# Where the split weights of paired pieces lie in their ring: 64 bytes below the plain ones, or 64 bytes above

## The reference

```
h = x @ w_up                                  # 2048 -> 2 * 5632
hc = conv_b + sum(conv_w[kk] * hp[:, kk:kk + S] for kk in range(3))
f = (silu(gate) * up) @ w_down                # 5632 -> 2048
x = layernorm(ALPHA * x + f)
```

## The kernel before

| operand | behind | at modulo 256 |
| --- | --- | --- |
| plain granules (`w_hi`, `w_lo`) | | 192 |
| `ffn_xT`, the moving operand of the feature stages | | 128 |
| `ffn_act`, `pairs_x`, `tokens_xT`, stationary in the token stages | a margin of 64 bytes | 192 |
| `next_held_w_hi/lo`, held granules | a margin of 64 bytes | 192 |
| `diff_split_...`, operands of the cross-attention in layer 1 | a margin of 64 bytes | 192 |
| `memory_memT` | margins of 64 and 192 bytes | 128 |
| `up_pair_w_hi/lo`, two granules kept apart | a margin of 64 and one of 32 bytes | 224 |

## Time and profile before

### The profile page before, as it was taken

How to read it: one execution, slowest core, us unless ns; L and a number is a source line. 1 busy time by engine, 2 the same in 40 slices (tenths; PEclk the granted TensorE clock), 3 DMA queues, 4 the chain that set the end, 5 groups by cost and what they waited for, 6 DMA issues and landing times.

```text
span 2082.7 us, 38940 instructions
## 1 busy us (share of the span) xinstructions
PE 2077.0 (100%) x14554; PEld 1916.0 (92%) x14554; DVE 1529.5 (73%) x2716; ACT 1215.3 (58%) x2222; POOL 2.7 (0%) x12
## 2 busy tenths in 40 slices
PE   9999999999999999999999999999999999999999
PEld 8999889999999998888888888899999999988887
DVE  6767777767766669888766558667766677688888
ACT  5645566556555555655656666566555565555654
POOL 0000000000000000000000000000000000000000
PEclk9999999999999999999999999999999999999999
DMA  9655666565655556556554454745655656565554
GB/s 348 235 176 167 210 219 213 188 201 181 201 190 192 196 176 212 183 201 223 192 168 165 167 177 167 256 153 193 201 192 191 198 185 198 169 218 181 204 202 162
DMA packets 201631, 408.97 MB, mean 196 GB/s; under 512 B 7616, under 2 KB 9152, under 8 KB 200768
## 3 DMA queue, kind: packets, MB, share of 16 engines
q1 hardware_dynamic: 201392, 407.45, 57.5%
q10 hardware_dynamic: 144, 0.26, 0.0%
HBM read 404.53 MB, written 3.15 MB: 196 GB/s over the span
## 4 chain that ended last, share of the span: by engine, by line
PE 98%; DVE 1%; DMA 0%; SPq 0%; ACT 0%; issue 0%
PE acc L1846 32%; PE acc L1848 32%; PE acc L1847 32%; PE acc L2177 0%; DMA head_first<-in_first 0%; PE acc L2151 0%; PE acc L1959 0%; PE acc L2201 0%; PE acc L1952 0%; PE acc L2209 0%; DVE x_tok L1817 0%; PE acc L2047 0%; SPq L563 0%; DVE x_tok L1822 0%; PE acc L2261 0%; PE acc L2282 0%
## 5 line engine op out<-in xcount | busy, mean ns | idle before, releaser
L1105 DVE TENSOR_TENSOR w_lo<-raw,w_hi 128x512 fp32r<-128x512 f32 x1330 | 878.5, 686 | 398.3 <-ACT w_hi L662 394.5
L662 ACT ACTIVATE w_hi<-raw 128x512 fp32r<-128x512 f32 x1330 | 804.6, 629 | 559.3 <-PE acc L1848 549.1
L1846 PE MATMUL acc<-ffn_xT,w_hi 128*128 128x256 f32 x2920 | 806.7, 276 | 0.0
L1847 PE MATMUL acc<-ffn_xT,w_hi 128*128 128x256 f32 x2920 | 806.2, 276 | 0.0
L1848 PE MATMUL acc<-ffn_xT,w_lo 128*128 128x256 f32 x2920 | 806.2, 276 | 0.0
L1847 PEld LDWEIGHTS acc<-ffn_xT,w_hi 128*128 128x128 f32 x2920 | 548.4, 188 | 0.1
L1846 PEld LDWEIGHTS acc<-ffn_xT,w_hi 128*128 128x128 f32 x2920 | 548.2, 188 | 0.1
L1848 PEld LDWEIGHTS acc<-ffn_xT,w_lo 128*128 128x128 f32 x2920 | 548.1, 188 | 0.0
L1846 PE MATMUL acc<-w_hi,ffn_act 128*128 128x512 f32 (+1 forms) x642 | 234.6, 365 | 0.0
L1847 PE MATMUL acc<-w_lo,ffn_act 128*128 128x512 f32 (+1 forms) x642 | 234.6, 365 | 0.0
L1848 PE MATMUL acc<-w_hi,ffn_act 128*128 128x512 f32 (+1 forms) x642 | 234.5, 365 | 0.0
(11 more groups left out here) (318 smaller groups left out, 1949.4 us busy)
## 6 DMA issues: line engine op xcount, KB each, us to landing
raw<-in_ffn_w_up SPq DMA_DIRECT2D x172, 1024.0 KB, 5.0
raw<-in_ffn_w_down SPq DMA_DIRECT2D x88, 1024.0 KB, 5.1
raw<-in_diff_w_in SPq DMA_DIRECT2D x38, 1024.0 KB, 5.4
raw<-in_w_out SPq DMA_DIRECT2D x32, 1024.0 KB, 5.1
raw<-in_pool_w_in SPq DMA_DIRECT2D x16, 1024.0 KB, 5.1
raw<-in_mem_w_kv SPq DMA_DIRECT2D x12, 1024.0 KB, 12.3
next_from_raw<-in_ffn_w_up SPq DMA_DIRECT2D x4, 1024.0 KB, 10.2
head_first<-in_first SPq DMA_DIRECT2D x5, 768.0 KB, 11.0
```

The costliest lines, as they stand in the source:

```text
L662: nc.scalar.activation(hi, raw_place(st, c, k, j), ACT.Copy).then_inc(hi_made, 1)
L1105: nc.vector.tensor_tensor(lo, raw_place(st, c, k, j), hi.bitcast(F32), ALU.subtract).then_inc(lo_made, 1)
L1846: pe.matmul(out, w[0], x[0], start=start, stop=False, skip_group_check=True)
L1847: pe.matmul(out, w[0], x[1], start=False, stop=False, skip_group_check=True)
```

## The change

Before, all units of a paired piece lie 64 bytes below the usual places, at 128 modulo 256, and so does the last plain granule in front of the piece, which would otherwise overlap the first unit. After, the first unit of a paired piece lies at the usual place (192), the six others 64 bytes above theirs (256, that is 0 modulo 256), and every plain granule at the usual place. The gap that stood ahead of the ring's first slot stands behind its last one. The size of the ring, the order of the instructions and their number on every engine stay the same; addresses and the counts in ACT's waits (`frees`) are what differs.

```
-SLOT_AT = [CHUNK * SLOT_ORDER.index(i) + 64 * sum(at in GAP_SLOTS for at in SLOT_ORDER[:SLOT_ORDER.index(i) + 1]) for i in range(HALVES * PIECE)]
+SLOT_AT = [CHUNK * SLOT_ORDER.index(i) + 64 * sum(at in GAP_SLOTS for at in SLOT_ORDER[1:SLOT_ORDER.index(i) + 1]) for i in range(HALVES * PIECE)]
...
-        self.places = [(SLOT_AT[(first + n + (skip if c > 0 else 0)) % len(SLOT_AT)] - (UNIT_SHIFT if self.lower(c, k, n - starts[c * pieces + k]) else 0))
+        self.places = [(SLOT_AT[(first + n + (skip if c > 0 else 0)) % len(SLOT_AT)] + (UNIT_SHIFT if self.higher(c, k, n - starts[c * pieces + k]) else 0))
...
-    def lower(self, c, k, j):
-
-        return self.paired(c, k) or (j == PIECE - 1 and k + 1 < self.pieces and self.paired(c, k + 1))
+    def higher(self, c, k, j):
+
+        return self.paired(c, k) and j > 0
```

## The result

| | before | after |
| --- | --- | --- |
| median of 20 runs, us | 2084.99 (2084.16 to 2086.72) | 2088.88 (2087.66 to 2089.98) |
| the profiled execution, its own time | 2084.49 | 2088.98 |
| its span | 2082.7 | 2087.2 |

The ratio is 1.0017, with a 95% interval of 1.0011 to 1.0024: 3.5 us slower (2.3 to 5.0); the medians in the table are 3.9 us apart. I had forecast 0.5 us faster. The time lies in the range of 8 in 10 that I gave but far outside the one around the forecast itself (2084.3 to 2086.1), and it is where the second rival put it (+3.2 us, 2088.8); the sign of the forecast was wrong.

What follows compares the result with a forecast made beforehand. PE was taken to bound the kernel, by matmul pace or a new wait. The terms -0.92 + 0.23 + 0.2 gave -0.5 us from 2085.57, so 2085.1 us (2084.3 to 2086.1); 8 in 10 range 2083.9 to 2091.1.

Steps and rivals of the forecast that it cites:

- the second rival: Paired pieces: units at 0 never fall into step behind a first unit at 120 ns; +3.2 us, 2088.8; chance 0.18.
- What bounds the kernel: Whole kernel: PE is busy throughout, so only the pace of matmuls or a new wait of PE can move the end.
- The last plain granule: Ahead of each pair, back from 128 to 192: 1.40 to 1.36 us, 23 times, 0.92 us less.
- The first unit: First six matmuls of each pair, from 128 to 192: 0.71 us against 0.70, 23 times, +0.23 us (0 to +0.5).
- The six other units: 828 matmuls in the pairs, from 128 to 0: pace taken as still 113.3 ns, 0 us; bounds -1.4 to +5.5.
- The seams: Switch from unit 0 to 1 and exit to a plain granule: 0.01 us per piece together, +0.2 us (-0.2 to +0.7).
- The waits of ACT: Some units in the ring written one use of PE later, others earlier; at the tightest place hidden by DVE's queue; 0 us.
- the first rival: Paired pieces: the units at 0 fall to 120 ns; +5.3 us, 2090.9; chance 0.20.
- The signs named in advance: Piece 0 of chunk 1: granule 1.36 us, first unit 0.71, 36 matmuls 4.08 and 276 ns in flight; longer means a rival.
- One sign against the mechanism: Stages outside the two `w_down` changing their pace would show the mechanism wrong, as would a plain granule keeping 1.40 at 192.

Runs made afterwards that it cites:

- the first experiment: Changed kernel with the six other units of each pair at 128 instead of 0, first units and waits as changed; median 2084.63 us, ratio 1.0001.
- second experiment: Changed kernel with the first unit of each pair at 0 as well, so all seven units at 0; 2088.84 us, ratio 1.0018.
- third experiment: Changed kernel with all seven units of a pair at 128 and every plain granule at 192; 2088.12 us, ratio 1.0015.
- kernel six: Changed kernel with unit places set by piece; in piece 3 the first unit at 192, the others at 96; one run, 2087.95 us.

## Why the prediction was wrong

**What bounds the kernel, and that only pace or a new wait can matter:** right. The loss is pace, 3.80 us of it inside the two `w_down`.

**The last plain granule, -0.92 us:** right, 1.40 to 1.36.

**The first unit, +0.23 us:** right in kind, 0.71 as the row of six matmuls at 192 in layer 1 had it, which is entered in the same way. The size was at the upper end of its bounds (0 to +0.5): the unit before takes 0.69 in most of the pieces, not the 0.70 of the piece that was shown, and the mean over the 23 goes from 0.692 to 0.713 us, 0.5 us in all.

**The six other units, 0 taken within -1.4 to +5.5:** this is the step that failed. I took 113.3 ns because 128 and 0 lie 64 bytes on either side of the stationary operand. That symmetry does not exist: at 0 the pace is 117.8, behind each of the four entries that were tried. 828 matmuls by 4.5 ns are 3.7 us, and the term had been put at nothing. The bounds held; the choice within them rested on no row.

**The seams, +0.2 us:** less than half of what was measured, and within its ends: by the means over the 23 pieces the exit goes from 1.375 to 1.393 us, 0.4 us in all, the granule behind it and the switch from the first unit to the second add 0.1 us or less each.

**The waits of ACT, 0:** right for PE, which had none in `w_down`; the first experiment kept all the counts and lost nothing. ACT's longest wait grew to 2.1 us, where I had named 1.0 us more at the tightest place.

**The second rival** had the pace (117.7, from the earlier trace rows) and nearly the sum, and the wrong reason; that its 2088.8 us and the measured 2088.88 agree is luck. Its +3.2 us, like the +5.3 of the first rival, leaves out the first unit's own +0.23. It said that the units at 0 stay out of step because of the 120 ns ahead of them. The same 120 ns ahead of units at 128 bring them *into* step, and units at 0 are at 117.8 with nothing of the kind ahead (second experiment). But what its row showed, two steady paces at one placement, is real, for 128: that row, and the 113.3 of the pairs, were the two.

**The kernel before owed its 113.3 to the granule that looked like a cost.** Its last plain granule at 128 takes 0.04 us more, and I counted its removal as the change's gain, which it is. But with the units at 128 it is also what sets their pace: without it they run at 117.7 (third experiment), 0.17 us per pair. A price and what it buys were read as if they were apart.

**The signs named in advance.** The plain granule at 1.36, the first unit at 0.71, 4.24 us for the 36 and 280 ns in flight are those of the second rival. One sign against the mechanism, a stage outside `w_down` that changes its pace, also came: the first stage did, but not by the change (last section).

By the rule of the Trainium skill ("TensorE: Matmul & The Clock Gate", Step-by-step) that the two operands have independent read ports, all eight kernels and both originals would have one time as far as PE goes; they span 2084.6 to 2090.7 us with the same number of instructions on every engine. What happens between the two operands inside the chip, the runs do not show.

**Open.** Whether the paces follow the distance between the two operands or the place of each: in the pairs the stationary one was at 192 throughout. The distance alone does not seem to fix them: stationary 224 with moving 128 runs at 120, stationary 192 with moving 96, the same 96 bytes apart, at 117.2 (kernel six); but they were entered differently, and 96 may have two paces as well. Nor does anything here show the addresses themselves: they come from the sizes in the source, and if the allocation began elsewhere, all places would move by the same amount. And what in the stream decides between 113.3 and 117.7; I have which entries lead where and no mechanism. Whether the accesses of ACT, DVE and the DMAs to the same memory have a part was not tested.

## What to carry to other kernels

Where PE is busy all the time, read its pace as the distance between starts for each form and each pair of addresses modulo 256: 4 to 7 ns of 113 are hidden in a busy share of 100%. Take a placement's pace only from a row with that very placement, reached through the same kind of matmul, since one placement can have two steady paces, and the first stage below shows that even this doesn't always settle which. Before an odd, seemingly dear arrangement is tidied, ask what the work right behind it does with it: here it was the entry.

## What the runs showed of the hardware that I had not expected

**Two steady paces at one placement.** 256 columns moving at 128 with the stationary operand at 192: 113.3 ns behind 512 columns at 128, or behind three, six or twelve matmuls of 256 at 192; 117.7 behind 512 columns at 192, and behind 256 at 0. In `w_down` each stays until the form or the place changes, up to 42 matmuls, and it was the same in all pieces with the same places and entry.

**The same in the first stage, and there it differs from run to run.** Early in the kernel 120 matmuls of 256 columns have `memT` moving at 128 and weights stationary at 192, the placement with the two paces. Behind them come 96 matmuls of 512 columns with the weights moving at 192 and `memT` stationary at 128. Starts halfway through the 120, at the first of the 96 and behind the last of them, before:

```profile
21.15 0.28 PE L1846 MATMUL acc<-memory_memT,w_hi 128*128 128x256 f32 x1
...
27.95 0.39 PE L1846 MATMUL acc<-w_hi,memory_memT 128*128 128x512 f32 x1
...
49.92 0.28 PE L1846 MATMUL acc<-memory_memT,w_hi 128*128 128x256 f32 x1
```

and after:

```profile
21.40 0.28 PE L1846 MATMUL acc<-memory_memT,w_hi 128*128 128x256 f32 x1
...
28.46 0.40 PE L1846 MATMUL acc<-w_hi,memory_memT 128*128 128x512 f32 x1
...
50.86 0.28 PE L1846 MATMUL acc<-memory_memT,w_hi 128*128 128x256 f32 x1
```

The last 60 of the 120 take 6.80 us before and 7.06 after (113.3 and 117.7 ns each), the 96 take 21.97 and 22.40 us (228.9 and 233.3 each). So the difference of 4.4 ns goes over from the one form to the other. For 120 and 96 matmuls it is 0.95 us, and that accounts for the 0.93 us by which after's execution was late at 833.28.

It is not the change that does this. The changed kernel and the eight derived from it have the same instructions at the same addresses in this stage; the traces of the first and the second experiment show the two quick paces of before, the other seven the two slow ones, and none shows a quick one beside a slow one. Another 96 matmuls of 512 columns with the same operands come later, from 72 us on, and take 229 ns in all ten traces. What decides between the paces here is open. It is likely a part of the spread of 2.6 us between runs of one kernel; that share was not measured.
